# Expert weights outside the ring: which ones, gathers for four experts at a time, and the order of the low-weight products

## The reference, cut to what matters

```python
def expert_block(args):                       # 32 experts in each of 2 layers
    xblk, e = args
    hid = jax.nn.silu(xblk @ w_gate[e]) * (xblk @ w_up[e])   # 1024 -> 512, twice
    return hid @ w_down[e]                                   # 512 -> 1024

def swiglu(x, w_in, w_out):                   # 4 times: 1024 -> 2 x 2816 -> 1024
    gate, up = jnp.split(x @ w_in, 2, axis=-1)
    return (jax.nn.silu(gate) * up) @ w_out
```

## Time and profile before

| | |
|---|---|
| median of 3 runs | 2577.12 us (2576.07 to 2582.03) |
| the profiled execution | 2576.62 us, span of its records 2574.8 us |
| PE busy | 2437.7 us, 95% |
| DVE, ACT, POOL busy | 54%, 34%, 12% |
| moved by DMA | 710.41 MB, mean 276 GB/s |
| granted TensorE clock | 0.992 of full speed |

### The profile page before, as it was taken

The page is one execution under the profiler, slowest core; times in us unless marked ns, Lnnn a source line. Parts: engine busy times, 40 slices in busy tenths (PEclk is TensorE's granted clock), DMA queues, the critical chain, the costliest instruction groups (busy, mean ns, idle before and its releaser), DMA issues.

```text
span 2574.8 us, 37020 instructions
## 1 busy us (share of the span) xinstructions
PE 2437.7 (95%) x14792; PEld 1740.7 (68%) x14793; DVE 1397.3 (54%) x2406; ACT 879.4 (34%) x1534; POOL 306.8 (12%) x371
## 2 busy tenths in 40 slices
PE   7999998988999998998899999999999999999998
PEld 4664433433686443443488899988888889998887
DVE  6564323222666332321276686667677678576666
ACT  2341111110342111110144465544444446555443
POOL 0210010000000010000000122340010012243001
PEclk8999999999999999999999999999999999999999
DMA  9988999999887799999938553453753755344371
GB/s 395 380 318 342 420 420 419 419 420 420 292 306 293 320 419 420 419 420 419 406 133 275 194 165 115 140 187 110 267 180 108 269 176 180 115 144 169 125 262 55
DMA packets 246335, 710.41 MB, mean 276 GB/s; under 512 B 11794, under 2 KB 165138, under 8 KB 189586
## 3 DMA queue, kind: packets, MB, share of 16 engines
q1 hardware_dynamic: 243810, 704.94, 72.1%
q10 hardware_dynamic: 2352, 3.06, 0.4%
HBM read 705.46 MB, written 1.05 MB: 274 GB/s over the span
## 4 chain that ended last, share of the span: by engine, by line
PE 70%; DMA 17%; DVE 5%; ACT 3%; issue 3%; POOL 1%; SPq 0%; DVEq 0%; ACTq 0%; POOLq 0%
DMA ring<-in_e_w_up_dram 14%; PE w L1289 11%; PE w L1049 11%; PE y L1058 10%; PE w L976 8%; PE w L1310 5%; PE w L1051 5%; PE w L979 4%; PE y L1345 2%; PE w L1559 2%; DVE wsp L1669 1%; DMA ring<-in_ffn_in_dram 1%; PE w L1263 1%; PE y L877 1%; ACT wsp L1659 1%
## 5 line engine op out<-in xcount | busy, mean ns | idle before, releaser
L1669 DVE TENSOR_TENSOR wsp<-ring,wsp 128x1024 fp32r<-128x1024 f32 x452 | 558.9, 1244 | 255.6 <-ACT wsp L1659 254.8
L1659 ACT CAST wsp<-ring 128x1024 fp32r<-128x1024 f32 x452 | 468.1, 1047 | 302.6 <-PE w L1049 106.6
L1289 PE MATMUL w<-ring,arena 128*64 128x512 f32 x1984 | 450.0, 598 | 74.1 <-DMA ring<-in_e_w_up_dram 67.9
L1049 PE MATMUL w<-hx,wsp 128*128 128x512 f32 x1344 | 475.2, 398 | 6.3 <-DVE wsp L1669 6.1
L1289 PEld LDWEIGHTS w<-ring,arena 128*64 128x64 f32 x1984 | 150.1, 137 | 335.9 <-issue 333.6
L1051 PE MATMUL w<-hx,wsp 128*128 128x256 f32 x1176 | 329.9, 281 | 0.0
L1049 PEld LDWEIGHTS w<-hx,wsp 128*128 128x128 f32 x1344 | 247.5, 188 | 58.0 <-DVE wsp L1669 8.2
L2188 DVE TENSOR_TENSOR ht<-w,ht 128x256 f32<-128x256 f32 x64 | 39.5, 617 | 428.8 <-ACT ht L2738 428.8
L976 PE MATMUL w<-hx,wsp 128*128 128x256 f32 x1984 | 264.9, 287 | 1.5 <-ACT arena L2827 1.0
L976 PEld LDWEIGHTS w<-hx,wsp 128*128 128x128 f32 x1984 | 247.1, 192 | 16.7 <-issue 12.2
L2738 ACT ACTIVATE ht<-w 128x256 f32<-128x256 f32 x64 | 40.0, 626 | 617.4 <-PE w L1289 617.4
(11 more groups left out here) (357 smaller groups left out, 2928.2 us busy)
## 6 DMA issues: line engine op xcount, KB each, us to landing
ring<-in_e_w_gate_dram SPq DMA_DIRECT2D x124, 1024.0 KB, 13.6
ring<-in_e_w_up_dram SPq DMA_DIRECT2D x124, 1024.0 KB, 15.7
ring<-in_e_w_down_dram SPq DMA_DIRECT2D x120, 1024.0 KB, 13.6
ring<-in_ffn_in_dram SPq DMA_DIRECT2D x88, 1024.0 KB, 6.3
ring<-in_ada_w_dram SPq DMA_DIRECT2D x48, 1024.0 KB, 14.8
ring<-in_w_in_dram SPq DMA_DIRECT2D x48, 1024.0 KB, 5.3
ring<-in_ffn_out_dram SPq DMA_DIRECT2D x44, 1024.0 KB, 6.3
ring<-in_b_w_in_dram SPq DMA_DIRECT2D x12, 1024.0 KB, 11.9
```

The lines of the kernel that those rows point to most:

```text
L1049: ins = pe.matmul(dst[:, :], wh[:, kc * P:(kc + 1) * P], hx[:, :, kc, :], start=kc == 0, stop=kc == KC - 1)
L1289: ins = pe.matmul(b[64 * c:64 * c + 64, :], xg[:, u, kc, x0:x0 + CAP], r4[:, k, :, 256 * c:256 * c + 256], start=kc == 0, stop=kc == KC - 1)
L1659: ac.copy(shaped(halves(i)[0], u.shape), u.cut(ring[:, u.piece % NSLOT, :])).then_inc(*mark("w_high", i))
L1669: ve.tensor_tensor(shaped(lo, u.shape), u.cut(ring[:, u.piece % NSLOT, :]), shaped(hi, u.shape).bitcast(F32), ALU.subtract).then_inc(*mark ...
```

## The change

1. `EARLY_UP` and `EARLY_DOWN` go. `ONCE = (0, 3, 9, 15)` takes their place: the down pieces of experts 0, 3, 9 and 15 lie outside the ring, again eight pieces in the same memory. All gate and up pieces and the other down pieces go through the ring.
2. Gathers are for groups of four experts (`GROUP = 4`, `SPAN = 256`), eight groups, one call of eight matmuls of 256 columns behind each turn of experts 0 to 27. `xg`, `Sg`, `Cg` hold half as many columns, which frees an area of `arena`. DVE makes `Sg` for the next group but one at every fourth expert.
3. The norm rows move from the turns of experts 3 to 6 to 10 to 13, the new `xa` waits for expert 12 and for the down pieces of expert 9, `add_residual` moves to e = 19.
4. `proj_wide` waits for `w_high` alone, does seven wide matmuls, then waits for `low_done`, does the eight narrow ones in a row, and the last wide one.

```diff
-EARLY_UP = 2
-EARLY_DOWN = 2
+ONCE = (0, 3, 9, 15)
+GROUP = 4
+SPAN = 256
...
-        early_up = (area(4864, 2, SLOT), early_h[:, :, :])
-        early_down = ((area(11008, SLOT), lnp[:, :, :].rearrange("p i d -> p (i d)")),
-                      (early_w[:, :], xa[:, :, :].rearrange("p t d -> p (t d)")))
+        once_at = {0: (area(11008, SLOT), early_h[:, 0, :]),
+                3: (early_h[:, 1, :], lnp[:, :, :].rearrange("p i d -> p (i d)")),
+                9: (xa[:, :, :].rearrange("p t d -> p (t d)"), area(4864, SLOT)),
+                15: (area(6912, SLOT), early_w[:, :])}
...
         def gathers_at(e_):
 
-            if e_ < 8:
-                return [(1, kc) for kc in {3: (0, 1), 4: (2, 3), 5: (4, 5), 6: (6,), 7: (7,)}.get(e_, ())]
-            return [(e_ // 8 + 1, e_ % 8)] if e_ // 8 + 1 < 4 else []
+            g = e_ // GROUP + 1
+            return [(g, e_ % GROUP)] if g < E // GROUP else []
...
-                for dst, src in early["down", l, 0]:
-                    sp.dma_start(dst, src).then_inc(*mark("in_down0", l, by=16))
-                for dst, src in early["up", l, 0]:
-                    sp.dma_start(dst, src).then_inc(*mark("in_up0", l, by=16))
+                for e_, h in ((0, 0), (3, 1), (9, 1), (15, 0)):
+                    load_once(l, e_, h)
...
             def early_second(l):
 
                 sp.wait_ge(*at("w_used", first["a_out" if l == 0 else "b_out"] + KC - 1))
-                for dst, src in early["up", l, 1]:
-                    sp.dma_start(dst, src).then_inc(*mark("in_up1", l, by=16))
-                for h, (dst, src) in enumerate(early["down", l, 1]):
-                    if h == 1:
-                        sp.wait_ge(*at("norm_v", "mix0" if l == 0 else "mix1", "added", 1, 1))
-                    sp.dma_start(dst, src).then_inc(*mark("in_down1", l, by=16))
+                load_once(l, 0, 1)
+                load_once(l, 3, 0)
+                load_once(l, 15, 1)
+                sp.wait_ge(*at("norm_v", "mix0" if l == 0 else "mix1", "added", 1, 1))
+                load_once(l, 9, 0)
...
             def proj_wide(dst, i):
 
                 wh, wl = halves(i)
-                pe.wait_ge(*low_done(i))
+                pe.wait_ge(*at("w_high", i))
                 for kc in range(KC):
                     if kc == KC - 1:
-                        pe.matmul(dst[:, 0:T], wl[:, kc * P:(kc + 1) * P], hh[:, kc, :], start=False, stop=False)
+                        pe.wait_ge(*low_done(i))
+                        for lc in range(KC):
+                            pe.matmul(dst[:, 0:T], wl[:, lc * P:(lc + 1) * P], hh[:, lc, :], start=False, stop=False)
                     ins = pe.matmul(dst[:, :], wh[:, kc * P:(kc + 1) * P], hx[:, :, kc, :], start=kc == 0, stop=kc == KC - 1)
-                    if kc < KC - 1:
-                        pe.matmul(dst[:, 0:T], wl[:, kc * P:(kc + 1) * P], hh[:, kc, :], start=False, stop=False)
                 ins.then_inc(*mark("w_used", i))
...
-                        if e_ < EARLY_DOWN:
-                            pe.wait_ge(*at(("in_down0", "in_down1")[e_], l))
-                            w = early_down[e_][h].rearrange("p (k n) -> p k n", k=2)
+                        if e_ in ONCE:
+                            pe.wait_ge(*at(f"in_once{e_}", l))
+                            w = once_at[e_][h].rearrange("p (k n) -> p k n", k=2)
```

More of the change, by code:

```diff
@@ L1239, in bank, with gather @@
                     return WB[i]
-                def gather_half(part, q):
-                    b = bank("xg_v" if q % 2 else "xg_s", l, "half", part, q)
+                def gather(g, q):
+                    u = g % 2
+                    b = bank("xg_v" if q % 2 else "xg_s", l, g, q)
                     if q == 0:
-                        pe.wait_ge(*at("chosen", "half", l, part))
+                        pe.wait_ge(*at("chosen", l, g))
                     for k in range(2):
@@ L1249, in gather_half @@
                             for j, a in enumerate((vh, vl)):
-                                if part == 0 and kc % 4 == 0:
+                                if g == 0 and kc % 4 == 0:
                                     pe.wait_ge(*(at("route_s", "v_hi", l, t, kc // 4) if j == 0 else at("v_lo", l, t, kc // 4)))
-                                ins = pe.matmul(b[:, T * k:T * k + T], a[:, t, kc * P:(kc + 1) * P], Sg[:, 0, t, T * part:T * part + T],
+                                ins = pe.matmul(b[:, SPAN * k:SPAN * k + SPAN], a[:, t, kc * P:(kc + 1) * P], Sg[:, u, t, :],
@@ L1253, in gather_half @@
                                                 start=t == 0 and j == 0, stop=t == 1 and j == 1)
[L1254 to L1265, removed]
+                    ins.then_inc(*mark("gathered", l, g, q))
@@ L1267, in up @@
                 def up(e_):
-                    g, u, x0 = e_ // 8, (e_ // 8) % 2, CAP * (e_ % 8)
+                    g, u, x0 = e_ // GROUP, (e_ // GROUP) % 2, CAP * (e_ % GROUP)
                     b = bank("hd", l, e_)
-                    if e_ and e_ % 8 == 0:
-                        pe.wait_ge(*at("xg_v", l, g, 7))
-                        pe.wait_ge(*at("xg_s", l, g, 6))
                     for h in range(2):
[L1274 to L1284, removed]
+                        if e_ % GROUP == 0:
+                            pe.wait_ge(*at("xg_s", l, g, 2 * h))
+                            pe.wait_ge(*at("xg_v", l, g, 2 * h + 1))
+                        for v in range(2):
+                            np_ = piece_of["up", l, e_, 2 * h + v]
+                            pe.wait_ge(*at(f"ring{np_ % NSLOT}", np_))
+                        two = ring[:, np_ % NSLOT - 1:np_ % NSLOT + 1, :]
@@ L1311, in down @@
                                                 start=h == 0 and c == 0, stop=h == 1 and c == 1)
-                        if e_ >= EARLY_DOWN:
+                        if e_ not in ONCE:
                             ins.then_inc(*mark("ring_read", np_))
-                    if e_ < EARLY_DOWN:
-                        ins.then_inc(*mark("ring_read", "early", "down", l, e_))
+                    if e_ in ONCE:
+                        ins.then_inc(*mark("ring_read", "once", l, e_))
                 def turn(e_):
@@ L1373, in moe @@
                 for q in range(4):
-                    gather_half(0, q)
+                    gather(0, q)
                 for e_ in range(E + 3):
@@ L1390, in moe @@
                         turn(e_)
-                        for g, kc in gathers_at(e_):
-                            gather(g, kc)
-                        if e_ < 4:
-                            gather_half(1, e_)
+                        for g, q in gathers_at(e_):
+                            gather(g, q)
                         if e_ == 0:
@@ L2136, in other_slots @@
                 def other_slots():
-                    for g in range(1, 4):
-                        v((f"sg{g}",), lambda: ve.tensor_scalar(sg[:, g, :], sg[:, 0, :], -512.0 * g, None, ALU.add))
+                    for g in range(2, E // GROUP):
+                        slots_of(g)
                 def many_tokens():
@@ L2522, in moe_banks @@
         def moe_banks(l):
-            order = [("half", 0, q) for q in range(4)]
+            order = [("gather", 0, q) for q in range(4)]
             for e_ in range(E + 3):
@@ L2533, in moe_banks @@
                         order.append(("weights", e_ // 2))
-                    order += [("gather", g, kc) for g, kc in gathers_at(e_)]
-                    if e_ < 4:
-                        order.append(("half", 1, e_))
+                    order += [("gather", g, q) for g, q in gathers_at(e_)]
                     if e_ == 0:
```

184 lines of the change are left out of this document (79 added, 105 removed).

## The result

The changed kernel takes 2540.0 us (median of 4 runs, 2537.38 to 2540.2) against 2576.9 us before: 36.9 us less, ratio 0.9849 with an interval of 0.9835 to 0.9863.

A forecast was written before the change was run, and what follows sets the result against it. DMA streaming of expert weights was taken to bound the expert stages, PE the feed-forward stages. Gains of 11.3 + 13.5 + 4.1 = 28.9 us from 2576.6 gave 2547.7, median 2548 us; range 2541 to 2560 (case A 2542 to 2559).

The forecast's parts named there:

- Rivals B and C: Expert stages: B, DMA gap comes back in part, 2558, chance 0.14; C, stage doesn't end on DMA, 2573, chance 0.06.
- Rival D: Expert stages: PE's clock falls to 1.2 GHz in bursts between waits, so the kernel gets slower; chance 0.03.
- The sum of the working: Expert stages: DMA gaps removed, gaining 11.3 us in layer 0 and 13.5 us in layer 1.
- the issue that the ring waited for: Layer 1, SP's queue: next ring piece issued at about 836.9 instead of 849.3 us, 12.4 us earlier.
- a cost of 0: Expert stages: extra gather time, +0.9 us of PE a layer, and smaller DVE and ACT steps hidden by DMA waits.
- the upper row: Feed-forward: neighbouring wide matmuls at 0.235 us each, input in two strips; a pair in runs 0.355, at most +6.7 us.
- +1 us: Feed-forward stages: cost taken for running wide and narrow matmuls in runs, between -3.4 and +6.7 us.
- The sign that I named: Feed-forward: prediction wrong if a run of narrow or wide matmuls has another spacing than 0.120 and 0.235 us.
- My lower bound of -3.4 us: Feed-forward order: wide matmuls with contiguous input at 0.2275 us give a pair of 0.3475, so -3.4 us.
- 3.6 + 1.5 = 5.1 us: Feed-forward waits saved: 0.9 us at each stage's start, 3.6 us in four, plus 1.5 us in mid stage.
- the 2.1 us of the list: Feed-forward: mid-stage part of PE's 6.1 us of listed waits for low weight parts; 1.5 counted as gained.
- the likeliest case: Case A, as worked out: 2548 us, experts gaining 20 to 27 us, feed-forward -3 to 9.5; chance 0.77.

The follow-up runs named there:

- the pieces of 0 to 3: Changed kernel with the down pieces of experts 0 to 3 outside the ring instead of 0, 3, 9 and 15: 2554.7 us.
- the expert part alone: Changed kernel with the old order and old waits in the feed-forward projections: 2547.2 us, ratio 0.9887.
- the kernel that waits first: Changed kernel with the wait for the low part back at the head of each projection, matmuls still in runs: 2543.0 us.
- the feed-forward part alone: Kernel before with the new proj_wide alone, its new order and new waits: 2568.5 us, ratio 0.9966.

## Why the prediction was off

*What bounds the kernel, and the expert stages: right.* Rivals B and C did not come true: no gap came back beyond 0.8 us, and the stages do end on DMA. Rival D had a trace of truth: the granted clock is 0.50 in two short stretches of layer 0's stage (606 to 609 and 637 to 640 us) and 0.99 over the whole of it, and the stage is 11.7 us shorter all the same. The sum of the working was 24.8 us, the stages are 25.4 us shorter. Layer 0: 11.3 said, 11.7 measured; layer 1: 13.5 said, 13.7 measured; the issue that the ring waited for moved by 12.4 us as counted. The gaps of DMA turned into time nearly one for one: 11.3 us of gap gone and 11.7 us gained in layer 0, 16.9 - 3.1 = 13.8 us gone and 13.7 gained in layer 1; going back, 4.8 and 8.6 us of gap cost 5.9 and 9.6 us with the pieces of 0 to 3. The first wait for data came inside 275 to 305 us. PE's waits for expert weights are 47.8 us, where I had 43 to 45. In one place a cost of 0 was a small gain: the even gathers closed the gap of 1.1 us, which I had put down to the ring alone.

*The feed-forward stages: the step that failed.* I wrote "I lean to the upper row" and "I take **+1 us**" for the order of the products. Measured, the order gains: the stages of the two kernels that wait for the low part first are 3.6 us shorter with runs than with alternation, a miss of 4.6 us and the largest part of the 8. A slice takes 8.307 us in place of 8.360; 84 times that would be 4.5, but the last slices of a stage, whose calls stand in another order with their rows, gain less. The error was in how I read the earlier trace rows. I took the 0.235 us of two neighbouring wide matmuls for the cost of a wide one in any surroundings, and explained it by the two strips of its input. But these two stand right behind narrow ones, where wide ones take 233 and 236 ns whatever their input: in the changed kernel the contiguous ones of `row` behind them are slow too (236, 228, 232 and 231 ns, then 227). From the sixth of a run on, the wide ones with two strips take 0.227 us, the same as the contiguous ones of the earlier trace rows, so the strips cost nothing. The sign that I named for this, another spacing than 0.235 in a run of wide ones, is what came. My lower bound of -3.4 us was worked out from the right row, and I gave it too little weight; that it comes so near to -3.6 is in part luck, since it counts no cost for the changes of kind, and its 0.350 us for a pair was read just behind the seam, where by medians a pair of the alternation takes 0.353.

*The waits.* 3.6 + 1.5 = 5.1 us said. At the start of the stages it was 0.9 us in each of the four, as worked out. In mid stage I had counted the 2.1 us of the list, and that was too little. By the slices, the one in each stage for which the weights come late (the eighth) takes 9.23, 9.70, 8.96 and 9.71 us before, with 0.5 us on two of the slices ahead of it, 4.7 us over the median in sum; in the kernel with the expert part alone it is 2.8 us, and after the change nothing is left but 0.15 us or less a stage at `row`. So the mid-stage waits gave 4.1 us against the profile of before and 2.3 beside the kernel that waits first, where I had said 1.5, and all waits together 7.8 or 5.8.

*The sum again.* 25.4 us from the experts, 3.6 from the order and some 7.8 from the waits, less 0.5 in all else, give 36.3 of the 36.4 us between the two profiled spans; the medians differ by 36.9. The 2.1 us by which the feed-forward stages of before and of the expert part alone differ are these mid-stage waits, and not the clock: no stretch at the lower level of 1.2 GHz lies in those stages, save at the very end of the program in both. The clock does show in the attention stages, which last 253.2 to 253.3 us or 254.6 to 254.8 in these traces, nothing between. Each of the seven long ones has a stretch of a few us in which the granted clock is 0.50 and none of the short ones has. One of them, in the profile of before:

```profile
2119.20:2373.80 254.60, 248.51 (x2093) 233.49 (x2092) 181.22 (x404) 142.26 (x307) 84.24 (x96) 0.99 0.47 154
2207.00:2210.00 3.00, 3.00 (x17) 3.00 (x16) 1.84 (x4) 1.22 (x3) 1.13 (x2) 0.50 0.84 249
```

*What stays open.* How late the weights come in mid stage: ACT's wait for the piece is 2.5 to 3.6 us in the profile of before and 2.5 to 4.3 in the kernel with the feed-forward part alone, and 2.2 to 3.1 in all kernels that have the groups of four. No run tells whether the expert part has a hand in this or chance. By medians the expert part alone is 29 us (25 to 33) and the feed-forward part 8 (6 to 12); the stage sums (24.9 to 25.4 and 8.9 to 11.5) lie in these or at their edge, and the intervals don't tell them apart further.

*The range.* The experts' 25.4 us lie inside the 20 to 27 of the likeliest case; the feed-forward stages' 11.5 us lie above its 9.5. The two best ends together would have been 27 + 9.5 = 36.5 us, thus 2540.6 and not the 2542 that I wrote, and nearly that is what happened.

## What to carry to other kernels

Where transfers set the pace, look for the windows in which the DMA engines stand still and ask which buffer slot they wait for: weights kept outside the ring should be ones that are read late, so that the first reads of the stage free slots of the ring, and it pays to free a place for that (here by smaller gather groups). A piece fewer ahead cost 2.5 us in layer 1 and 1.3 to 1.8 in layer 0, so count it by the gaps that DMA then has. For a change of order on PE, take the spacing from a row with the same neighbours on both sides, several deep; two matmuls at a seam don't give the price of a run. Count mid-stage waits by the length of the whole slice, not by the list of waits alone. And a wait for a by-product can be pushed behind work that doesn't need it.

## What the runs showed of the hardware that I had not expected

With operands of type fp32r and new weights at each matmul, 512 columns take 227 ns and 256 columns 120 ns deep in runs of their kind. In strict alternation they take 236 and 117 ns, a sum of 353 against 347. In pairs the sum is 350. A single change of kind is felt for five wide matmuls: behind a run of narrow ones they take 233, 236, 228, 232 and 231 ns and then 227, while the first narrow one behind a wide one takes 113, so a change and back costs some 18 ns. An input in two strips of 256 columns is as quick as a contiguous one of 512, and a switch of the PSUM bank costs nothing either (227 ns ahead of it).
